# Values of a dilated head pair moved behind the second projection, which is split around the second half of the next pair's scores

## The reference, cut to what matters

```python
z = h @ w_in
cq, ck, cv, rq, rk, rv, rg = jnp.split(z, cuts, axis=-1)
yc = dilated_mixture(cq, ck, cv, pos)          # 8 heads of 64
yr = retention(rq, rk, rv, pos)                # 4 heads of 128
yd = jax.nn.silu(rg) * yr
return jnp.concatenate([yc, yd], axis=-1) @ w_out
```

## Time and profile before

| | |
|---|---|
| median of 3 runs | 1391.12 us (1391.07 to 1391.23) |
| the profiled execution, its own time | 1390.97 us |
| its span, first to last instruction | 1389.2 us |
| granted TensorE clock, mean | 0.999 of full speed |
| TensorE busy | 1379.5 us (99%) |
| VectorE, ScalarE, GpSimd busy | 64%, 46%, 8% |
| the four dilated pairs | about 720 to 817 us of the span |

### The profile page before, as it was taken

The page is one execution under the profiler, slowest core; times in us unless marked ns, Lnnn a source line. Parts: engine busy times, 40 slices in busy tenths (PEclk is TensorE's granted clock), DMA queues, the critical chain, the costliest instruction groups (busy, mean ns, idle before and its releaser), DMA issues.

```text
span 1389.2 us, 20696 instructions
## 1 busy us (share of the span) xinstructions
PE 1379.5 (99%) x8090; PEld 1215.4 (87%) x8090; DVE 889.9 (64%) x1240; ACT 640.6 (46%) x953; POOL 107.9 (8%) x90
## 2 busy tenths in 40 slices
PE   9999999999999999999999999999999999999997
PEld 8988888889999998888887788988888999998887
DVE  6656556479888883334578755765559887885332
ACT  6632534354545552322756634544454545554221
POOL 0012200110000000100111211100020000000000
PEclk9999999999999999999999999999999999999999
DMA  9721320222323233334221212542132232323321
GB/s 356 254 91 61 106 91 31 91 91 82 116 92 122 92 109 126 101 117 139 94 89 47 83 39 78 189 144 77 46 106 91 92 116 98 108 106 121 107 76 61
DMA packets 42136, 147.16 MB, mean 106 GB/s; under 512 B 5056, under 2 KB 5568, under 8 KB 42048
## 3 DMA queue, kind: packets, MB, share of 16 engines
q1 hardware_dynamic: 38448, 136.46, 28.7%
q10 hardware_dynamic: 3600, 9.45, 1.9%
HBM read 143.80 MB, written 2.10 MB: 105 GB/s over the span
## 4 chain that ended last, share of the span: by engine, by line
PE 96%; DVE 2%; issue 1%; ACT 1%; DMA 0%; POOLq 0%; POOL 0%; ACTq 0%; DVEq 0%
PE acc L1857 19%; PE acc L1859 19%; PE acc L1858 19%; PE acc L2195 7%; PE acc L2196 7%; PE acc L2197 7%; PE acc L1905 3%; PE acc L1906 3%; PE acc L1907 3%; PE aux L2197 1%; PE aux L2195 1%; PE aux L2196 1%; PE acc L2275 1%; PE aux L2263 1%; PE aux L1859 0%
## 5 line engine op out<-in xcount | busy, mean ns | idle before, releaser
L1131 DVE TENSOR_TENSOR w_lo<-raw,w_hi 128x1024 fp32r<-128x1024 f32 x181 | 224.9, 1244 | 215.1 <-ACT w_hi L578 214.8
L578 ACT ACTIVATE w_hi<-raw 128x1024 fp32r<-128x1024 f32 x181 | 190.0, 1053 | 186.0 <-PE acc L1859 146.9
L1857 PE MATMUL acc<-act_hi,w_hi 128*128 128x512 f32 (+1 forms) x374 | 141.6, 379 | 0.0
L1859 PE MATMUL acc<-act_hi,w_lo 128*128 128x512 f32 (+1 forms) x374 | 140.9, 377 | 0.0
L1858 PE MATMUL acc<-act_lo,w_hi 128*128 128x512 f32 (+1 forms) x374 | 140.9, 377 | 0.0
L1857 PE MATMUL acc<-u_hi,w_hi 128*128 128x512 f32 x352 | 138.8, 394 | 0.0
L1859 PE MATMUL acc<-u_hi,w_lo 128*128 128x512 f32 x352 | 137.2, 390 | 0.0
L1858 PE MATMUL acc<-u_lo,w_hi 128*128 128x512 f32 x352 | 137.1, 389 | 0.0
L1056 POOL TENSOR_TENSOR sqsum<-sqsum,tmp 128x512 f32<-128x512 f32 x41 | 53.1, 1295 | 976.6 <-ACT tmp L587 976.6
L2195 PE MATMUL acc<-b_hi,s_hi 128*128 128x256 f32 x432 | 122.5, 283 | 0.0
L2197 PE MATMUL acc<-b_hi,w_lo 128*128 128x256 f32 x432 | 122.3, 283 | 0.0
(11 more groups left out here) (251 smaller groups left out, 3221.7 us busy)
## 6 DMA issues: line engine op xcount, KB each, us to landing
raw<-in_weights SPq DMA_DIRECT2D x253, 512.0 KB, 3.3
hT<-in_x_t ACTq DMA_DIRECT2D x4, 512.0 KB, 7.4
x_tok<-in_x ACTq DMA_DIRECT2D x4, 512.0 KB, 4.8
raw<-in_weights SPq DMA_DIRECT2D x5, 256.0 KB, 5.9
mem_tok<-in_mem ACTq DMA_DIRECT2D x2, 512.0 KB, 5.8
out_h<-out_f SPq DMA_DIRECT2D x2, 512.0 KB, 2.6
memT<-in_mem_t SPq DMA_DIRECT2D x3, 256.0 KB, 6.1
out_h<-out_tok ACTq DMA_DIRECT2D x1, 640.0 KB, 3.5
```

The source lines that it names most:

```text
L578: act.activation(w_hi[:, s, :], raw[:, s, :], ACT.Copy).then_inc(hi_ready, 1)
L1131: dve.tensor_tensor(w_lo[:, s, :], raw[:, s, :], w_hi[:, s, :].bitcast(F32), ALU.subtract)\
L1857: pe.matmul(out, w_h, x_h, start=first, stop=False)
L1859: return pe.matmul(out, w_l, x_h, start=False, stop=last)
```

## The change

It touches three pairs of four (p = 0, 1, 2). On TensorE the second side unit is cut into halves of 12 matmuls; the first half goes between the two parts of the next pair's scores, the second half behind them, and the values come after it, before the third side unit. On ScalarE `y_hi` of the values moves from ahead of the second weight split and the exponentials to behind the second unit's partner rows. On VectorE `y_lo` moves from between the two groups of maxima to behind the drain of the second unit, ahead of the first head's `normalise`. The accumulator numbers of the values and of the second unit are swapped. Pair 3 keeps its order. No instruction of an arithmetic kind is added or removed.

```diff
 def pair_places(p):
-    return [(3 * p + n, 4 * p + c) for n, c in enumerate((0, 2, 3))], 4 * p + 1
+    own = 1 if p == DIL_H // 2 - 1 else 2
+    return [(3 * p + n, 4 * p + c) for n, c in enumerate((0, 3 - own, 3))], 4 * p + own
...
# ScalarE
                     side(first)
-                    act.wait_ge(acc_done, t + 1)
-                    y_hi_part(p, accs[t % 4][:, :])
+                    if p == DIL_H // 2 - 1:
+                        act.wait_ge(acc_done, t + 1)
+                        y_hi_part(p, accs[t % 4][:, :])
                     side_split(second)
...
                         exps(2 * p + 2)
                         exps(2 * p + 3)
                     side(second)
+                    if p + 1 < DIL_H // 2:
+                        act.wait_ge(acc_done, t + 1)
+                        y_hi_part(p, accs[t % 4][:, :])
                     side_split(third)
...
# VectorE
                         maxima(p + 1, 0)
-                    y_lo_part(p, acc(t)[:, :], PHM1 + p + 1, acc_drained)
+                    if p + 1 == DIL_H // 2:
+                        y_lo_part(p, acc(t)[:, :], PHM1 + p + 1, acc_drained)
                     if p + 1 < DIL_H // 2:
                         maxima(p + 1, 1)
                     side(second)
+                    if p + 1 < DIL_H // 2:
+                        y_lo_part(p, acc(t)[:, :], PHM1 + p + 1, acc_drained)
                     if p + 1 < DIL_H // 2:
                         normalise(2 * p + 2)
...
# TensorE
                     if p + 1 < DIL_H // 2:
                         scores(p + 1, (0, 1))
-                    values(p)
-                    if p + 1 < DIL_H // 2:
+                        half_side(second, 0)
                         scores(p + 1, (2, 3))
+                        half_side(second, KT // 2)
+                        values(p)
                     else:
+                        values(p)
                         pe.wait_ge(rot_ready, 16)
                         for h in range(RET_H):
                             turn_keys(h)
-                    side(second)
+                        side(second)
```

## The result

| | before | after |
|---|---|---|
| median of 10 runs | 1391.05 us | 1394.93 us |
| range of the runs | 1390.75 to 1391.23 | 1394.85 to 1395.24 |
| span of the profiled execution | 1389.2 us | 1393.5 us |

The change costs 3.88 us; the ratio is 1.0028, 95% interval 1.002 to 1.0037. The forecast was 3.45 us.

What follows compares the result with a forecast made beforehand. TensorE, busy 1379.5 of 1389.2 us, bounds the kernel. Switches and wait, 3 x (0.42 + 0.73) = 3.45 us, take the median from 1391.12 to 1394.57; range 1392.4 to 1395.7, the forecast's own 1393.9 to 1395.4.

Steps and rivals of the forecast that it cites:

- the switches: TensorE passing from one kind of matmul to another in three pairs: 0.42 us a pair, 1.26 us for three.
- (a): TensorE's own work: same matmuls, new neighbours; halves of 2.93 us each, third unit 5.58; 0.42 us extra a pair.
- (b): First head's probabilities: `y_lo` at 12.83 after about 2.0 us of VectorE wait, ready at 14.90, transposes due 15.18, in time.
- (c): Second head's probabilities: multiplications from 17.95, ready 19.23, transposes due 19.05; with 0.14 hand-over, 0.32 us of TensorE wait.
- (d): GpSimd's addition holds the second head's multiplications 0.41 us, to its end at 18.36; TensorE's wait becomes 0.73 a pair.
- the rival in which the multiplications pass freely: Second head's multiplications not held by GpSimd's addition; 0.32 wait, copies add 0.2 in two pairs: 2.6 us, 1393.7, chance 0.17.
- What else moves: Weight transfers, later splits and values' bank drain: no cost; the wait does not grow from pair to pair.

Runs made afterwards that it cites:

- e1: Changed kernel, but VectorE takes `y_lo` behind the first head's `normalise`, no longer ahead of it: 1392.5 us, ratio 1.0011 to the kernel before.
- e2: Changed kernel, but ScalarE takes `y_hi` ahead of the second unit's partner rows: 1392.41 us, ratio 1.0009 to the kernel before.
- e5: The change made in pair 2 alone, pairs 0 and 1 as in the kernel before: 1391.98 us, ratio 1.0007 to the kernel before.
- e4: Changed kernel, but GpSimd's additions for the eight side units cover 16 of 512 columns: 1393.62 us, ratio 1.0019 to the kernel before.
- e3: Changed kernel, but ScalarE copies the first head's transposed probabilities ahead of the third unit's partner rows: 1393.94 us, ratio 1.002 to the kernel before.

## Why the prediction was right

Both costs that it named are there: the switches, and the second head's transposes late behind VectorE's multiplications. A third cost was missing. That the sum still came near (3.45 for 3.88) is in part luck: the missing cost and one that was sized too large went against each other.

- **(a) TensorE's own work.** Forecast 0.42 a pair, measured 0.44 (15.20 for 14.76); e1, e2 and e5 show it with no wait beside it. The place that no row of before had, the entry from the values, costs what the entry from scores does: the third unit took 769.35 - 763.77 = 5.58.
- **(b) The first head.** Every start in the chain was met within 0.02 us (in brackets the forecast): `y_lo` at 12.83 (12.83), VectorE's wait 1.96 (2.0), multiplications at 13.64 (13.62). The transposes were in time.
- **(c) The second head.** The drain, the reciprocal and the start of the multiplications came as reckoned (17.97 for 17.95). The hand-over to TensorE was less: the work ended at 773.63, the first transpose began at 773.69, 0.06 and not the 0.14 of the earlier trace rows.
- **(d) GpSimd in the way.** The direction was right, and e4 shows the cause; the size was off. The multiplications lost 0.23 and not 0.41. The first one takes 0.29 when nothing is beside it (763.59 in the trace before), so the first, ended at 772.64, was really under way from about 772.35, 0.2 us before the addition's end as shown. The weight split of the earlier trace rows says the same: 2.14 less 1.21 is 0.93 of wait, and from its start to the addition's end it was 1.06. With 0.23 and 0.06, the wait forecast as 0.73 becomes 0.47, and 0.47 was measured. By the Trainium skill (SBUF — State Buffer, on the port pair shared by VectorE and GpSimd) whoever starts first has the pair for its whole instruction. The trace agrees that the one behind is held, and for these multiplications too; but they go on 0.2 us before the addition's shown end, the weight split 0.13, so the shown end was the wrong point to count the wait to.
- **The step that was missing.** I let the copies wait only in the rival in which the multiplications pass freely, since in the forecast the transposes came so late that the copies (from 19.16) would be ahead of them. I had the third unit's partner rows start at VectorE's drain. They also wait for GpSimd's addition of the unit two before, which I had taken for that of the unit just before (772.65 - 754.15 = 18.50 and not 17.86), so the copies began at 19.80, and with them came 0.58 of wait in two pairs. e3 takes this away but for 0.06 a pair. The missing wait made up in the sum for the two sizes that were too large: 3 x 0.73 = 2.19 was forecast as wait, 3 x 0.47 + 2 x 0.58 = 2.57 came.
- **What else moves.** Nothing came from the weight transfers, and the wait did not grow: from first transposes to first transposes it is 24.14, 24.97 and 24.96 us for 23.69, 23.44 and 23.45 before. I had forecast 1.15 more for each of the three. The first of these distances has only the switches (0.45), since each wait comes behind the first head's transposes and so falls into the distance after; the last wait lies behind all three.

## What to carry to other kernels

Where TensorE's queue has no gap, a reordering can't gain, and it should be priced by two things: whole measured blocks with their entries and exits, and the slack of each wait that stands later in the queue. A short instruction that waits (here `y_lo`, 0.6 us of work) is dangerous for what stands behind it in its queue: with 2 us of wait on a half-idle VectorE and scores that came 0.6 us later, 0.3 of 2.5 us of slack was left at one head and none at the next, which had had 1.5 (ready at 768.48 + 1.28, wanted at 771.26). When the slack is gone, follow each waiting engine's semaphores once more, and look up in the code which unit each one counts; the second wait had been hidden behind slack that the first one used.

## What the runs showed of the hardware

- A GpSimd addition holds up a VectorE multiplication of one SBUF operand by a per-row factor: 0.52 us instead of 0.29 beside it, 1.51 instead of 1.28 for the four, and 1.27 again with the addition narrowed. Worked out from these, the multiplication gets going some 0.2 us before the addition's shown end. All runs that show it have nearly the same overlap (0.42 to 0.44 us), so whether it stands still or runs slower is not shown for it.
- For the weight split it is a standstill: where it began 1.06, 1.16 (e3) and 0.25 us (the rows below, before) ahead of the end of a GpSimd addition, it took 0.93, 1.04 and 0.12 us more than the usual 1.21, each time 0.12 or 0.13 less than the overlap.

```profile
772.06 1.33 DVE L1131 TENSOR_TENSOR w_lo<-raw,w_hi 128x1024 fp32r<-128x1024 f32 x1 [1.11 <-ACT w_hi L578]
```

```profile
771.03 1.28 POOL L1102 TENSOR_TENSOR tq<-tq,tmp 128x512 f32<-128x512 f32 x1 [2.70 <-DVE tmp L1661]
```

- Entering a run of 512-column matmuls costs TensorE the same 0.14 us from values as from scores (5.58 for 5.44 us of a unit).
- From VectorE's last write to TensorE's first transpose it took 0.06 us (e3 and e4 as well), from ScalarE's first copy to the transposes that waited for it 0.05 (774.55 to 774.60), and in the earlier trace rows, also from ScalarE, 0.14. So it is not the releasing engine that makes the difference; what does stays open.
- Ten transposes that begin after a wait took 1.07 us to the next half unit, ten that wait for nothing 1.01 (the gate's pair after; e3 and e5 within 0.01).
